# Attention units in three parts on TensorE, and the low halves of every third mixer weight panel on GpSimd

## What is computed

```python
h = rms_norm(x, norm_mix[layer])
(u_pool, q, kv, qi, ki, wi, u_conv, z, xbc, dt_raw, gate_logits) = jnp.split(h @ w_in, offsets, axis=-1)
...
logits = jnp.einsum('bqgrd,bqkgd->bqgrk', qg, ks).astype(jnp.float32) * scale
p = jax.nn.softmax(logits, axis=-1)
o = jnp.einsum('bqgrk,bqkgd->bqgrd', p, vs)
...
u = jnp.einsum('bsnc,ncd->bsnd', branches, w_br)
merged = jnp.einsum('bsnd,bsnd->bsd', gates, u)
x = x + merged @ w_out
```

## Time and profile before

| | |
|---|---|
| median of 3 runs | 1969.56 us (1968.22 to 1969.62) |
| the profiled execution's own time | 1960.89 us |
| its span, first to last instruction | 1959.1 us |
| mean granted TensorE clock | 0.967 |
| busy: PE, DVE, ACT, POOL | 94%, 78%, 58%, 0% |
| mixer of layer 0, mixer of layer 1 | about 0 to 364 us, 560 to 914 us |

### The profile page before, as it was taken

One profiled execution on the slowest core, in us unless ns is written; L12 is line 12 of the kernel. 1 busy time (PEld: TensorE's weight loads), 2 busy tenths in 40 slices (PEclk: granted clock), 3 DMA queues, 4 the chain that ended last, 5 costly groups with the idle time before them and its releaser, 6 DMA issues.

```text
span 1959.1 us, 28204 instructions
## 1 busy us (share of the span) xinstructions
PE 1842.4 (94%) x10776; PEld 1622.6 (83%) x10776; DVE 1521.7 (78%) x1487; ACT 1131.3 (58%) x925; POOL 5.1 (0%) x13
## 2 busy tenths in 40 slices
PE   6999889899989998897899999999999999999996
PEld 6989878799979988786788888888888888888884
DVE  3979957545448789766788989889898898988985
ACT  3335554443433265544577767777677776777764
POOL 0000000000000000000000000000000000000000
PEclk9999999999988899999899999999999999999997
DMA  6435334665334334345599999999999999999991
GB/s 231 147 113 165 119 105 132 231 206 181 127 112 152 119 130 148 111 132 202 177 381 337 360 357 364 356 349 361 367 352 358 348 359 379 342 361 342 358 377 66
DMA packets 232259, 485.50 MB, mean 248 GB/s; under 512 B 16992, under 2 KB 41568, under 8 KB 232048
## 3 DMA queue, kind: packets, MB, share of 16 engines
q1 hardware_dynamic: 231120, 479.65, 69.2%
q0 software_dynamic: 1056, 4.70, 0.6%
HBM read 483.24 MB, written 1.05 MB: 247 GB/s over the span
## 4 chain that ended last, share of the span: by engine, by line
PE 81%; DVE 12%; ACT 4%; issue 1%; DMA 1%; SPq 0%; DVEq 0%; ACTq 0%
PE pair L815 56%; PE aux L815 19%; DVE lo_ring L1308 3%; PE aux L1199 2%; PE pair L1221 1%; ACT hi_ring L432 1%; PE aux L1272 1%; DMA raw_ring<-in_w_in 1%; DVE arena L1540 1%; DVE arena L1489 1%; DVE arena L1475 1%; DVE small L1488 1%; DVE pair L1465 0%; DVE arena L1554 0%; ACT arena L477 0%
## 5 line engine op out<-in xcount | busy, mean ns | idle before, releaser
L1308 DVE TENSOR_TENSOR lo_ring<-raw_ring,hi_ring 128x2048 fp32r<-128x2048 f32 (+2 forms) x278 | 623.3, 2246 | 146.1 <-ACT hi_ring L432 144.2
L432 ACT ACTIVATE hi_ring<-raw_ring 128x2048 fp32r<-128x2048 f32 (+2 forms) x278 | 522.5, 1881 | 304.3 <-PE pair L815 221.9
L1308 DVE TENSOR_TENSOR lo_ring<-arena,hi_ring 128x2048 fp32r<-128x2048 f32 x183 | 417.6, 2289 | 99.0 <-ACT hi_ring L432 97.4
L432 ACT ACTIVATE hi_ring<-arena 128x2048 fp32r<-128x2048 f32 x183 | 350.3, 1918 | 152.6 <-PE aux L815 81.4
L815 PE MATMUL pair<-hT_lo,hi_ring 128*128 128x256 f32 x1328 | 389.5, 293 | 22.7 <-DVE lo_ring L1308 7.9
L815 PE MATMUL pair<-lo_ring,hT_hi 128*128 128x512 f32 (+3 forms) x992 | 382.3, 385 | 3.9 <-DVE hT_lo L1813 2.4
L815 PE MATMUL pair<-hT_hi,lo_ring 128*128 128x256 f32 x1328 | 383.7, 289 | 0.0
L815 PE MATMUL pair<-hT_hi,hi_ring 128*128 128x256 f32 x1328 | 383.2, 289 | 0.0
L815 PE MATMUL pair<-hi_ring,hT_hi 128*128 128x512 f32 (+3 forms) x992 | 377.9, 381 | 0.0
L815 PE MATMUL pair<-hi_ring,hT_lo 128*128 128x512 f32 (+3 forms) x992 | 377.4, 380 | 0.0
L815 PEld LDWEIGHTS pair<-hT_lo,hi_ring 128*128 128x128 f32 x1328 | 262.8, 198 | 30.4 <-ACT arena L477 9.7
(11 more groups left out here) (278 smaller groups left out, 1886.8 us busy)
## 6 DMA issues: line engine op xcount, KB each, us to landing
raw_ring<-in_mu SPq DMA_DIRECT2D x222, 512.0 KB, 5.7
arena<-in_mg SPq DMA_DIRECT2D x220, 512.0 KB, 5.2
raw_ring<-in_w_in SPq DMA_DIRECT2D x120, 512.0 KB, 4.5
arena<-in_md SPq DMA_DIRECT2D x114, 512.0 KB, 5.4
raw_ring<-in_md SPq DMA_DIRECT2D x110, 512.0 KB, 5.4
raw_ring<-in_w_br SPq DMA_DIRECT2D x32, 512.0 KB, 4.5
raw_ring<-in_w_out SPq DMA_DIRECT2D x16, 512.0 KB, 4.3
raw_ring<-in_fg SPq DMA_DIRECT2D x12, 512.0 KB, 4.0
```

Source lines behind the costliest of these rows:

```text
L432: nc.scalar.activation(hi_ring[:, h, 0:cols], raw(slot)[:, 0:cols], ACT.Copy).then_inc(hi_ready, 1)
L1308: nc.vector.tensor_tensor(lo_ring[:, h, 0:cols], raw(slot)[:, 0:cols], hi_ring[:, h, 0:cols].bitcast(f32), ALU.subtract).then_inc(lo_ready, 1)
```

## The change

1. GpSimd makes the low halves of panels 8, 11, 14, ... 44 of each mixer (13 of 46) and counts them in a semaphore of its own, `lo_by_pool`. DVE leaves them out. PE and SP wait for the one or the other counter (`lo_of`). All panels of slot 2 from panel 8 on are GpSimd's.
2. The probabilities and the turned probabilities have two places each. On PE a unit is cut into three parts that run one step apart: `logits(u)`, `turn_probs(u - 1)`, `attend(u - 2)`. ACT's copies follow with the same distance. Unit 7 is turned, and units 6 and 7 attended, behind panel 33, which moves ahead of the products of B and C.

```diff
+POOL_LO = [i for i in range(MIX_PANELS) if i % 3 == 2 and i > 5]
+MIX_DVE_LO = MIX_PANELS - len(POOL_LO)
...
+        PROBS = (A_CACC + 512, A_P + 1536)
+        PROBS_T = (A_YPAD, A_YPAD + 512)
...
+        def lo_of(L, i):
+
+            if i in POOL_LO:
+                return lo_by_pool, L * len(POOL_LO) + POOL_LO.index(i) + 1
+            return lo_ready, MIX_LO[L] + i + 1 - sum(1 for q in POOL_LO if q < i)
...
                     if slot in last:
-                        sp.wait_ge(lo_ready, last[slot] + 1)
+                        sp.wait_ge(*last[slot])
                     halves(slot, width, src)
-                    last[slot] = p
+                    last[slot] = lo_of(L, i)
...
+            def low_halves(L):
+                for i in POOL_LO:
+                    slot, _ = MSLOT[L][i]
+                    p = MIX_BASE[L] + i
+                    pool.wait_ge(hi_ready, p + 1)
+                    nc.gpsimd.tensor_tensor(lo_ring[:, p % HRING, 0:cols[i]], raw(slot)[:, 0:cols[i]],
+                                            hi_ring[:, p % HRING, 0:cols[i]].bitcast(f32), ALU.subtract).then_inc(lo_by_pool, 1)
+
+            gain_load(0)
+            pool.dma_start(params[:, :], params_d[0, :, :]).then_inc(param_in, 16)
+            pool.dma_start(consts[:, 128:], consts_d[:, 128:]).then_inc(const_in, 16)
+            gain_load(1)
+            low_halves(0)
+            pool.wait_ge(*ev(0, "br3h1"))
+            pool.dma_start(params[:, :], params_d[1, :, :]).then_inc(param_in, 16)
+            gain_load(2)
+            gain_load(3)
+            low_halves(1)
+            gain_load(4)
...
                 def probs_out(u):
                     j, b = u % 4, u // 4
                     act.wait_ge(S["probs_turned"], 8 * L + u + 1)
+                    if u > 1:
+                        act.wait_ge(S["attended"], 8 * L + u - 1)
                     n = 2 * (b + 1) * 128
-                    nc.scalar.activation(ar(A_YPAD, n), aux[:, 1024:1024 + n], ACT.Copy).then_inc(S["probs_copied"], 1)
+                    nc.scalar.activation(ar(PROBS_T[u % 2], n), aux[:, 1024:1024 + n], ACT.Copy).then_inc(S["probs_copied"], 1)
...
-                    act.wait_ge(S["attended"], 8 * L + u + 1)
+                    act.wait_ge(S["attended"], 8 * L + max(u + 1, 8 if u == 6 else 0))
...
                     if u:
-                        att_out(u - 1)
-                    probs_out(u)
+                        probs_out(u - 1)
+                    if u > 1:
+                        att_out(u - 2)
...
+                probs_out(7)
+                att_out(6)
                 att_out(7)
...
                 def panel(width, body):
-                    pe.wait_ge(lo_ready, p[0] + 1)
+                    pe.wait_ge(*lo_of(L, p[0] - MIX_BASE[L]))
...
+                def turn_probs(u):
+                    j, b = u % 4, u // 4
+                    nb = b + 1
+                    pe.wait_ge(S["probs_done"], 8 * L + u + 1)
+                    if u:
+                        pe.wait_ge(S["probs_copied"], 8 * L + u)
...
                 def attend(u):
...
                     pe.wait_ge(S["probs_copied"], 8 * L + u + 1)
-                    if b:
-                        pe.wait_ge(S["att_copied"], 8 * L + j + 1)
+                    if u:
+                        pe.wait_ge(S["att_copied"], 8 * L + min(u, 6))
...
                     logits(u)
                     beside[u]()
-                    attend(u)
+                    if u:
+                        turn_probs(u - 1)
+                    if u > 1:
+                        attend(u - 2)
...
                 pe.wait_ge(S["xbc_done"], L + 1)
+                pe.wait_ge(S["logits_read"], 8 * (L + 1))
...
                 ins.then_inc(S["xs_turned"], 1)
+                t_panel("g1h1", 1)
+                turn_probs(7)
+                attend(6)
+                attend(7)
                 pe.wait_ge(S["att_copied"], 8 * (L + 1))
...
-                t_panel("g1h1", 1)
...
-                        to_lo(p, slot, MCOLS[i], p % HRING)
+                        if i not in POOL_LO:
+                            to_lo(p, slot, MCOLS[i], p % HRING)
```

More of the change, by code:

```diff
@@ L341, in _ @@
             for i in range(DENSE_PANELS):
-                last[i % FRING] = DENSE_BASE + i
+                last[i % FRING] = (lo_ready, DENSE_LO + i + 1)
             mixer(1)
-            sp.wait_ge(lo_ready, EXP_BASE)
+            sp.wait_ge(lo_ready, EXP_LO)
+            sp.wait_ge(lo_by_pool, 2 * len(POOL_LO))
             sp.wait_ge(*ev(1, "br3h1"))
@@ L405, in _, with gain_load @@
             pool.dma_start(consts[:, 0:128], consts_d[:, 0:128]).then_inc(ident_in, 16)
-            for n in range(5):
+            def gain_load(n):
                 if n:
@@ L584, in exps @@
                     for r in range(2):
-                        ins = nc.scalar.activation(ar(A_CACC + 512 + r * 256, w), ar(A_CACC + r * 256, w), ACT.Exp,
+                        ins = nc.scalar.activation(ar(PROBS[u % 2] + r * 256, w), ar(A_CACC + r * 256, w), ACT.Exp,
                                                    bias=ar(A_MISC + 96 + r, 1), accum_out=ar(A_MISC + 98 + r, 1))
@@ L993, in logits @@
                     ins.then_inc(S["logits_done"], 1)
+                def turn_probs(u):
[4 more added lines that the diff above has]
+                        pe.wait_ge(S["probs_copied"], 8 * L + u)
+                    for r in range(2):
+                        for s in range(nb):
+                            o = 1024 + (r * nb + s) * 128
+                            ins = pe.transpose(aux[:, o:o + 128], ar(PROBS[u % 2] + r * 256 + s * 128, 128), C("ident"))
+                    ins.then_inc(S["probs_turned"], 1)
                 def attend(u):
```

38 lines of the change are left out of this document (15 added, 23 removed).

## The result

The changed kernel takes 1984.30 us (median of 8 runs, 1976.51 to 1989.22); the kernel before, run beside it, takes 1968.28 us (8 runs, 1960.28 to 1970.16). The ratio is 1.0093 with a 95% interval of 1.0068 to 1.0117: **slower by about 18 us**. The profiled execution of the changed kernel is its longest, 1989.22 us with a span of 1987.4; that of before was among its shortest, 1960.89. So the 28 us between the two traces hold some 10 us that the medians do not, and the first table of stretches shows where these lie.

The account below looks back on a forecast made before the run. PE is busy 94% of the span, and DVE paces the attention units. Terms of +4.75 us in layer 0 and +6.05 in layer 1 give +10.8, added to the 1969.56 median: 1980.4 us; overall range 1954 to 1992, own range 1973 to 1992.

Parts of the forecast that it names:

- One sign that the prediction named against itself: In the attention units, a granted PE clock other than the 0.96 of before would count as wrong.
- The subtract at 4.4 us: One low half on GpSimd takes 4.4 us, twice DVE's 2.2; low end 2.29, high end 5.7.
- It holds DVE for its whole length: GpSimd's subtract shuts out DVE's two-operand SBUF instructions throughout, costing DVE up to 4.4 us where it saved 2.2.
- GpSimd has a way of its own: Rival: GpSimd reads SBUF without holding any DVE instruction; together -13.1 us, 1956.5 us; chance 0.32.
- Convolution +2.0: Layer 0's convolution: held taps end at 129.4 where PE asks at 127.4, +2.0 us; layer 1: 0.
- DVE goes first: Rival: gapless convolution taps keep GpSimd out, so its 4.4 us subtracts delay PE; 1987 to 2005 us; chance 0.12.
- the rule that it quotes: Skill note: two-SBUF-input DVE instructions and SBUF-reading GpSimd instructions shut each other out for their whole length, by issue order.
- Panel 20, +1.6 and +2.1: GpSimd makes panel 20 late for PE, because a DVE instruction goes first: +1.6 us in layer 0, +2.1 in layer 1.
- Units, 6.05 held against 6.6 saved, -0.55 each: Attention units: panels 26, 29, 32 hold DVE 6.05 us but relieve it of 6.6, so -0.55 us per layer.
- Three parts, -3.0 and -0.2: From the last logits read to the decay rows, the three-part unit shortens layer 0 by 3.0 us, layer 1 by 0.2.
- Panel 38 +3.1, panel 44 +1.6 per layer: GpSimd delays the masking of head 3 by 3.1 us and the merged branches' low half by 1.6, both awaited by PE.
- The gate of unit 2, 1.0 us: ACT's gate of unit 2 delays unit 3's exponentials by 1.0 us, hidden where GpSimd already holds DVE.

Follow-up runs that it names:

- experiment 5: The changed kernel with only panels 38 and 44 made on GpSimd: 1978.23 us, ratio 1.0070 to the kernel before.
- experiment 4: The changed kernel with only panels 8, 11 and 14 made on GpSimd: 1962.69 us, ratio 0.9999 to the kernel before.
- experiment 6: The changed kernel with only panels 20, 26 and 32 made on GpSimd: 1971.28 us, ratio 1.0031 to the kernel before.
- experiment 1: The changed kernel with no panel on GpSimd, attention units still in three parts: 1964.14 us, ratio 1.0000 to the kernel before.
- experiments 8 and 12: The changed kernel with panel 33 split in two on PE; GpSimd makes panels 23, 29, 35, 41 (8: 1956.58 us) or none (12: 1955.32 us).
- experiment 2: The kernel before with only GpSimd's thirteen panels added, units still in two parts: 1994.14 us, ratio 1.0169 to the kernel before.

## Why the prediction was right, and where its steps were off

The sign, the size and the mechanism came out: 1980.4 us forecast, 1984.3 measured, inside the forecast's own range of 1973 to 1992. The sum was +10.8 us; measured are 16 by the medians and 18 by the ratio, and 24 by the stretches of one trace pair. So the sum was too small, and part of the closeness is luck: one term was 2.0 us too high, which covered part of what four others had too low. One sign that the prediction named against itself appeared as well: the granted clock of the units was 0.93 and 0.92 in place of 0.96, and no term held that.

- *The subtract at 4.4 us*: 4.50 to 4.62. Right.
- *It holds DVE for its whole length*: right where GpSimd has got in (taps, L1475, L1660). "GpSimd has a way of its own" is refuted by L1660, 3.68 us in place of 0.55, and by experiment 5, where two panels a layer cost 14 us.
- *Convolution +2.0*: 0 (experiment 4). The step took every subtract as holding DVE. DVE's taps kept GpSimd out, until a low half of DVE's had ended (panel 8, at 60.9), until DVE idled (panel 11, at 87.8), and for panel 17 until the taps had ended at 126.4. So the turns did not go by who came first, as the prediction and the rule that it quotes ("by order of issue") had it. It was a piece of the rival "DVE goes first", without its price, because PE's panels were not due yet.
- *Panel 20, +1.6 and +2.1*: the stretch grew by 3.2 and 3.5, experiment 6 has 3.3 and 2.2. Of that 2.4 is PE's wait for GpSimd; I had PE arrive 0.8 us later than it does.
- *Units, 6.05 held against 6.6 saved, -0.55 each*: +0.7 and +2.1 (82.7 and 84.1 against 82.0 with the cut alone), and panels 26 and 32 alone make +1.3 and +1.5. The failed step is that only two-operand instructions were taken as held: L1545 and L1564, one tensor each, took 2.95 and 2.93 us, so 2.7 and 2.8 were lost where 2.5 and 2.2 were forecast. Panel 29 was right (1.4 us held). The three holds are 6.9 us against 6.6 saved; the rest of the stretch's growth goes with the lower clock and is not explained by a hold.
- *Three parts, -3.0 and -0.2*: -3.5 and -0.7 up to the decay rows, as worked out, the gap of 2 to 3 us being 1.9. What the step left out is what mostly comes behind the gap: in experiment 1 2.5 and 2.2 us, by a lower clock (0.50 just behind it). With that term the cut is worth nothing, which experiment 1 shows, and experiments 8 and 12 take it back. Nor did the sum hold what experiment 2 shows, that the cut is worth 5.3 and 3.6 us when DVE is being held.
- *Panel 38 +3.1, panel 44 +1.6 per layer*: PE's waits grew by 3.1 and 1.7. As waits these are exact. As time they made 5.8 and 7.0 us together (experiment 5) against 4.7, and the difference is PE being slower behind them.
- *The gate of unit 2, 1.0 us*: no wait in the changed units points at it.

So the terms that I sized too low have mostly one thing in common: a stall of PE was priced at its length, and the stretches grew by the length and some 1 to 2.5 us of slower clock. That the stall brings the slower clock is shown for the gap ahead of the decay rows (14 of 16 places with it, none of eight without); for the stalls at panels 20, 38 and 44 it is read from PE's busy time alone.

## What to carry to other kernels

Work moved to an idle engine is not free of the engine that it was taken from: look at which of that engine's instructions would meet it, and allow it only in stretches whose instructions don't collide or whose end nobody waits for; here eight of 26 moved panels cost nothing, and four made 14 us. Cutting the moved instruction smaller shortens each hold but gives the other engine more occasions to keep it out. And before you judge a reordering by the waits that it removes, look for the gap that it opens elsewhere: the same cut was worth 0 us with a gap of 1.9 us ahead of short matmuls, and 13 us by the medians (9 by the stretches of the traces) once half a panel of work stood in it.
